# Reordering the first layer: turned output in bank O, memory prepared in steps, branch jobs inside the memory attention, another opening

## The chip, the cores and the metric

The kernel runs on one core of one Trainium2 chip. Its time is the device time of one execution in microseconds (us), and the time before is the median of three runs. Five things of a core matter here: TensorE (PE) multiplies into PSUM banks, VectorE (DVE) and ScalarE (ACT) move and transform data, and the queues of SyncE (SP) and ScalarE issue the DMAs. Each engine takes its instructions strictly in the order in which they were issued to it, and engines wait for each other through semaphores.

## The reference

A transformer block is followed by two layers of another kind, for 512 tokens of width 1024 in float32. The change touches the first block alone:

```python
h = rms_norm(x, norm_mix)
aq, ak, av, bq, bk, bv, cq = split(h @ w_in)            # heads normed, but for the values
out_a = rms_norm(diff_attention(aq, ak, av, slopes_a, lam), a_subln) * (1 - lambda_init)
out_b = softmax-weighted sum of three dilated_window_attention(bq, bk, bv)
m = rms_norm(mem, mem_norm); ck, cv = split(m @ w_mem_kv); ck = rms_norm(ck)
out_c = memory_attention(rms_norm(cq), ck, cv)          # 256 memory tokens
branches = einsum(stack([out_a, out_b, out_c]), w_branch)
gates = sigmoid(h @ w_gate + b_gate)                    # 3 x 1024 columns
x = x + sum(gates * branches) @ w_out
x = x + (silu(h2 @ w_ffn_gate) * (h2 @ w_ffn_up)) @ w_ffn_down
```

## The kernel before

Every large product is made of three matmuls on split operands (high x high, high x low, low x high; `three`, lines 912 to 914). Weights come in units of eight 128x128 tiles (512 KB) through a ring of four buffers. SyncE loads them (L883), ScalarE copies the high part (`whi`, `high`, L1216), VectorE subtracts for the low part (`wlo`, `low`, L1441), and `open_units` puts these two steps into the order two units ahead of their use.

The order of all work is one list, made by hand in `build_schedule` (from L232). Each engine's program walks through that list and issues what the step means to it, so the order of the list is the order of each engine's queue. A step that means nothing to an engine is passed over. A `job` is one column of 128 outputs for all tokens (24 matmuls, 12 for a branch job), in one of three banks, followed by its evacuation `evac` on VectorE. A `group` makes four columns at once for tokens as rows, in four parts (`gpart`, 24 matmuls for x and 12 for the memory), then `gevac`, squares `gsq`, `ginv`, `gnorm`, and the turning `gturn` by PE into bank T0 or O, out of which ScalarE copies. `flush` runs what was deferred after each part or job.

`attend` runs an attention as tiles of 128 queries: `score` (PE, maximum on VectorE, exponential on ScalarE), `probs` (VectorE), `turn` (transposes into T0, copied out by ScalarE) and after four tiles `pv` into bank O. `spread` divides other work, given as pieces, over two slots per tile. The first attention (A) has 16 tiles; its output of each head is normed and turned as a group of its own, `g=("AO", h)`, into `OAH` and `OAL`. Then come the first branch's jobs, the second attention (B), the memory's preparation (`memload`, eight `memfresh`), the second branch (eight jobs with six gate jobs between them), keys and values of the memory (`c_keys`, `c_values`), the memory attention (C) with seven gate jobs as its pieces, the third branch, the reload of x, and `w_out`.

`free[slot]` says for each bank which event a writer has to wait for. For a turned output of attention A it is the end of its low half (L1573), which VectorE writes after ScalarE's high half; for T0 in `turn` it is ScalarE's copy; for O in `pv` it is whatever used O last. The gates' sigmoid (L1340), the exponential (L1355, L1362) and the root (L1305) each load ScalarE's table anew where the function changes.

In the opening, `setup` is the first step: ScalarE issues five constants; PE multiplies a small product of VectorE; then `enter` splits x chunk by chunk (`XH` on ScalarE, `XL` on VectorE, L1489).

## Time and profile before

| | |
|---|---|
| median of 3 runs | 3383.36 us (3381.9 to 3385.7) |
| profiled execution | 3380.15 us |
| its span | 3378.4 us |
| mean granted clock of TensorE | 0.992 |
| busy: PE, VectorE, ScalarE | 3269.1, 1720.1, 1116.2 us |
| HBM read | 309.58 MB, 92 GB/s over the span |

The span runs from the first to the last instruction of the profiled execution. A busy time is the sum over an engine's instructions. In the timeline and the waits, what stands in brackets is how long the engine had been idle before the instruction, and the instruction that released it. The edited places lie in the first 770 us: the opening (0 to 37), the attention A (92 to 262), the second branch (526 to 582), the memory attention (613 to 691), the third branch and `w_out` (691 to 768).

### The profile page before, as it was taken

The numbers are of one execution on the slowest core, as the hardware profiler recorded it, in microseconds if no ns is written. First come the engines' busy times: TensorE is split into PE (matmuls) and PEld (weight loads), VectorE is DVE, ScalarE is ACT, GpSimd is POOL, SyncE is SP. The second block draws the span as 40 slices with busy tenths as digits, with TensorE's granted clock in tenths as the row PEclk, the third lists the DMA queues.
The fourth block names the chain that finished last, engine by engine and source line by source line (L and its number), as shares of the span: only waits on it lengthen the run. The fifth ranks groups of instructions, "written<-read, shape, count | busy, mean of one in ns | idle before, by whom it ended". The sixth has DMA issues, their size and how long they took to land.

```text
span 3378.4 us, 40341 instructions
## 1 busy us (share of the span) xinstructions
PE 3269.1 (97%) x15218; PEld 2683.1 (79%) x15218; DVE 1720.1 (51%) x2485; ACT 1116.2 (33%) x1723; POOL 0.2 (0%) x4
## 2 busy tenths in 40 slices
PE   8899999889999999999999999999999989999998
PEld 7677777678888888888886888888888878688887
DVE  6554445555444445346654545344543666554543
ACT  4554543533222222232333322232223233332221
POOL 0000000000000000000000000000000000000000
PEclk9999999999999999999999999999999999999999
DMA  4223222232222222232221223222223223122222
GB/s 140 94 82 100 92 77 88 87 106 94 96 97 98 96 94 98 96 113 69 88 94 50 99 94 99 94 97 96 97 95 111 80 75 100 63 84 97 97 96 87
DMA packets 88538, 313.43 MB, mean 93 GB/s; under 512 B 9952, under 2 KB 10464, under 8 KB 87904
## 3 DMA queue, kind: packets, MB, share of 16 engines
q1 hardware_dynamic: 82080, 294.69, 26.2%
q10 hardware_dynamic: 6336, 17.03, 1.6%
q8 instruction: 87, 1.43, 0.2%
q14 instruction: 35, 0.29, 0.0%
HBM read 309.58 MB, written 2.10 MB: 92 GB/s over the span
## 4 chain that ended last, share of the span: by engine, by line
PE 90%; DVE 4%; ACT 3%; issue 2%; DMA 1%; DVEq 0%; ACTq 0%; SPq 0%
PE ps L912 28%; PE ps L914 27%; PE ps L913 27%; PE ps L1170 1%; PE ps L1085 1%; ACT stage_sq L1297 1%; PE ps L1063 1%; PE ps L1117 1%; ACT whi L1216 1%; PE ps L1074 1%; PE ps L1100 0%; PE ps L1121 0%; PE ps L1200 0%; PE ps L976 0%; DVE wlo L1441 0%
## 5 line engine op out<-in xcount | busy, mean ns | idle before, releaser
L912 PE MATMUL ps<-x_hi,whi 128*128 128x512 f32 x2400 | 947.5, 395 | 5.0 <-DVE gate_sb L1608 3.5
L914 PE MATMUL ps<-x_hi,wlo 128*128 128x512 f32 x2400 | 937.8, 391 | 0.0
L913 PE MATMUL ps<-x_lo,whi 128*128 128x512 f32 x2400 | 937.8, 391 | 0.0
L1216 ACT ACTIVATE whi<-raw 128x1024 fp32r<-128x1024 f32 x554 | 583.1, 1055 | 969.2 <-DMA raw<-in_weights 966.2
L1441 DVE TENSOR_TENSOR wlo<-raw,whi 128x1024 fp32r<-128x1024 f32 x554 | 676.4, 1223 | 414.8 <-ACT whi L1216 406.5
L912 PEld LDWEIGHTS ps<-x_hi,whi 128*128 128x128 f32 x2400 | 453.3, 189 | 104.0 <-issue 5.2
L914 PEld LDWEIGHTS ps<-x_hi,wlo 128*128 128x128 f32 x2400 | 452.8, 189 | 95.4
L913 PEld LDWEIGHTS ps<-x_lo,whi 128*128 128x128 f32 x2400 | 453.0, 189 | 94.8 <-issue 2.2
L912 PE MATMUL ps<-h_hi,whi 128*128 128x512 f32 x880 | 342.3, 389 | 0.0
L913 PE MATMUL ps<-h_lo,whi 128*128 128x512 f32 x880 | 342.3, 389 | 0.0
L914 PE MATMUL ps<-h_hi,wlo 128*128 128x512 f32 x880 | 342.3, 389 | 0.0
L1725 DVE TENSOR_TENSOR ffn_u<-ps,rstd_x 128x512 f32<-128x512 f32 x110 | 76.0, 691 | 474.7 <-PE ps L914 474.7
L914 PEld LDWEIGHTS ps<-h_hi,wlo 128*128 128x128 f32 x880 | 165.2, 188 | 34.3
L912 PEld LDWEIGHTS ps<-h_hi,whi 128*128 128x128 f32 x880 | 165.2, 188 | 34.3
L913 PEld LDWEIGHTS ps<-h_lo,whi 128*128 128x128 f32 x880 | 165.2, 188 | 34.2
L912 PE MATMUL ps<-whi,x_hi 128*128 128x512 f32 x416 | 168.3, 405 | 3.6 <-DVE wlo L1441 3.2
L1255 ACT ACTIVATE sq<-x_res 128x512 f32<-128x512 f32 x88 | 55.4, 631 | 351.9 <-DVE x_res L1592 301.6
L914 PE MATMUL ps<-whi,x_lo 128*128 128x512 f32 x416 | 163.2, 392 | 0.0
L913 PE MATMUL ps<-wlo,x_hi 128*128 128x512 f32 x416 | 163.0, 392 | 0.0
L1408 ACT ACTIVATE ffn_s<-ffn_g 128x512 f32<-128x512 f32 x110 | 69.6, 632 | 216.2 <-DVE ffn_g L1723 216.2
L1592 DVE SCALAR_TENSOR_TENSOR x_res<-ps,x_res 128x512 f32<-128x512 f32 x72 | 49.8, 691 | 161.1 <-PE ps L914 154.2
L912 PEld LDWEIGHTS ps<-whi,x_hi 128*128 128x128 f32 x416 | 78.9, 190 | 29.2 <-issue 9.3
(274 smaller groups left out, 3415.4 us busy)
## 6 DMA issues: line engine op xcount, KB each, us to landing
raw<-in_weights SPq DMA_DIRECT2D x554, 512.0 KB, 3.3
bias<-in_biasB ACTq DMA_DIRECT2D x16, 384.0 KB, 3.2
bias<-in_biasA ACTq DMA_DIRECT2D x16, 256.0 KB, 3.1
mem_raw<-in_mem ACTq DMA_DIRECT2D x3, 1024.0 KB, 7.5
x_res<-in_x SPq DMA_DIRECT2D x8, 256.0 KB, 6.9
x_res<-in_x ACTq DMA_DIRECT2D x1, 2048.0 KB, 9.5
out_x<-x_res SPq DMA_DIRECT2D x8, 256.0 KB, 2.0
pool_w_sb<-in_pool_w ACTq DMA_DIRECT2D x2, 256.0 KB, 4.9
```

Of the source, the lines that this page charges most:

```text
L912: pe.matmul(out, hi, xhi, start=start, stop=False)
L913: pe.matmul(out, hi, xlo, start=False, stop=False)
L914: return pe.matmul(out, lo, xhi, start=False, stop=stop)
L1063: mm = pe.matmul(sc[:, c * T:(c + 1) * T], AQ[r, h, tt], AK[r, h, :], start=True, stop=True)
L1074: mm = pe.matmul(sc, XQ[:, 2 * h + c, tt], XK[:, 2 * h + c, :], start=(c == 0), stop=(c == 1))
L1085: mm = pe.transpose(out, probs(a)[:, c * P:(c + 1) * P], ident[:, :])
L1216: return act.activation(out, in_, ACT.Copy, scale=scale)
L1255: act.activation(SQ[:, a["sq"], :], X[:, m, :], ACT.Square).then_inc(*sig("sq", (n, m)))
L1408: act.activation(FS[:, :], FG[:, :], ACT.Silu).then_inc(sems["silu"], 1)
L1441: dve.tensor_tensor(wlo[u % RING][:, :], raw[u % RING][:, :], whi[u % RING][:, :].bitcast(F32), ALU.subtract).then_inc(sems["unit_ready"], 1)
L1592: dve.scalar_tensor_tensor(X[:, m, :], out, a["c"], X[:, m, :], ALU.mult, ALU.add)\
L1725: dve.tensor_tensor(FU[:, :], PS[:, 2 * jj + 1, :], RSTD[:, :], ALU.mult).then_inc(sems["fu"], 1)
```

## The change

- The output of attention A is turned in bank O instead of T0.
- Opening: `opening` comes first (ScalarE issues `cols`, VectorE writes zeros, PE makes three matmuls on them), the first unit is loaded and split in halves, and the first part of the first group takes all four token tiles of the first half before those of the second. The constants `ones`, `ident` and `poolrec` are issued at `enter` 3, `halves` is gone, and `setup` stands after the first part.
- The memory's eight `memfresh` steps are put in pairs between the first jobs of the second branch, with gate jobs 2 to 5.
- The second half of the second branch (jobs 4 to 7, gate jobs 6 and 7) becomes four more pieces of the memory attention, before the gate jobs 0 to 6 of the third; gate job 7 follows the attention, and gate job 0 no longer stands before it.
- In the third branch the low half of `y` is its own step `ylo`, one job later.

```diff
 
         def turns():
-            for slot in ("T0", "O"):
+            for slot in ("O", "T0") if isinstance(a["g"], tuple) else ("T0", "O"):
                 if turned:
                     self.step("gturn", c=turned.pop(0), slot=slot, **a)
...
 
-    step("setup")
-    for u, chunks in enumerate(((0,), (1, 2, 3), (4, 5))):
+    step("opening")
+    step("enter", m=0, gain="norm_mix")
+    step("halfunit")
+    step("enter", m=1, gain="norm_mix")
+    s.open_units(0)
+    for u, chunks in ((1, (2, 3)), (2, (4, 5)), (2, (6, 7))):
         for m in chunks:
             step("enter", m=m, gain="norm_mix")
         s.open_units(u)
-    for m in (6, 7):
-        step("enter", m=m, gain="norm_mix")
     a_keys[0]()
     step("consts")
+    step("setup")
     for m in range(4):
         step("refresh", n=0, m=m, gain="norm_mix", entered=True)
...
 
-    def branch(n, o, gate_dst, gates_done):
-        for jj in range(DC // 2):
-            if not gates_done and jj:
-                for m in (2 * jj, 2 * jj + 1):
-                    gate_chunk(n, m, gate_dst(m))
-            t0 = len(s.units) * UT
-            s.unit("w_branch", n, [(k, 2 * jj + mm) for mm in range(2) for k in range(4)])
-            for mm in range(2):
-                m = 2 * jj + mm
-                need = {k: [("olo", ("ABC"[n], k))] for k in range(4)} if m == 0 else {}
-                s.job(t0 + 4 * mm, 4, rhs=o, n=T, evac="branch", b=n, m=m, need=need, gate=gate_dst(m))
+    def branch_pair(n, o, gate_dst, jj):
+        t0 = len(s.units) * UT
+        s.unit("w_branch", n, [(k, 2 * jj + mm) for mm in range(2) for k in range(4)])
+        for mm in range(2):
+            m = 2 * jj + mm
+            need = {k: [("olo", ("ABC"[n], k))] for k in range(4)} if m == 0 else {}
+            s.job(t0 + 4 * mm, 4, rhs=o, n=T, evac="branch", b=n, m=m, need=need, gate=gate_dst(m))
+            if n == 2 and m:
+                step("ylo", m=m - 1)
 
 
     for go in gates_a[5:]:
         go()
     s.drain()
-    branch(0, "OA", lambda m: ("Y", m), True)
+    for jj in range(DC // 2):
+        branch_pair(0, "OA", lambda m: ("Y", m), jj)
     b_work = [b_parts[12:20], b_parts[20:28], b_parts[28:37], b_parts[37:] + [lambda m=m: gate_chunk(1, m, ("GT", m)) for m in range(2)]]
     for h in range(NHEAD):
         attend(b_tiles[h], b_work[h])
...
 
-    for go in memory(0, 0, "mem_norm"):
+    def gate_b(m):
+        gate_chunk(1, m, ("GT", m % 2))
+
+    def pair_b(jj):
+        branch_pair(1, "OB", lambda m: ("GT", m % 2), jj)
+
+    memload, *memparts, memsum = memory(0, 0, "mem_norm")
+    memload()
+    pair_b(0)
+    for k, go in enumerate((lambda: gate_b(2), lambda: gate_b(3), lambda: pair_b(1), lambda: gate_b(4))):
         go()
-    norms, s.norms = s.norms, []
-    branch(1, "OB", lambda m: ("GT", m % 2), False)
-    s.norms = norms
+        memparts[2 * k]()
+        memparts[2 * k + 1]()
+    memsum()
+    gate_b(5)
     gates_c = [lambda m=m: gate_chunk(2, m, ("GC", m)) for m in range(DC)]
-    gates_c[0]()
     attend([dict(kind="C", h=h, t=t, need=[("hq", ("CQ", h)), ("hq", ("CK", h))], need_v=[("gev", (c_group, NM // P - 1))])
-            for h in range(NHEAD) for t in range(NT)], gates_c[1:])
-    branch(2, "OC", lambda m: ("GC", m), True)
+            for h in range(NHEAD) for t in range(NT)],
+           [lambda: pair_b(2), lambda: gate_b(6), lambda: gate_b(7), lambda: pair_b(3)] + gates_c[:7])
+    gates_c[7]()
+    for jj in range(DC // 2):
+        branch_pair(2, "OC", lambda m: ("GC", m), jj)
+    step("ylo", m=DC - 1)
     step("reload")
     norm = 1
...
                 sp.dma_start(X[:, m, :], dram["x"][:, m, :]).then_inc(d_x[m], 16)
-                if m % 2:
+                if m == 0:
+                    sp.dma_start(raw[0][:, 0:4 * P], dram["weights"][0, :, 0:4 * P]).then_inc(sems["d_half"], 16)
+                elif m == 1:
+                    sp.dma_start(raw[0][:, 4 * P:8 * P], dram["weights"][0, :, 4 * P:8 * P]).then_inc(raw_landed[0], 16)
+                elif m % 2:
                     load(0, m // 2)
             with sp.Fori(1, NU // RING) as i:
...
             for kind, a in SCHEDULE.steps:
-                if kind == "setup":
-                    pe.wait_ge(sems["d_cols"], 32)
+                if kind == "opening":
+                    pe.wait_ge(*on("setup", "zeros"))
+                    for _ in range(3):
+                        pe.matmul(O, GSQ[:, 0, 0:P], GSQ[:, 0, :], start=True, stop=True)
+                elif kind == "setup":
...
                     xhi, xlo = parts[a["rhs"]]
-                    pe.wait_ge(sems["unit_ready"], a["unit"] + 1)
-                    for t in range(a["nt"]):
+                    if a["unit"] == 0:
+                        pe.wait_ge(*on("half_ready"))
+                    else:
+                        pe.wait_ge(sems["unit_ready"], a["unit"] + 1)
+
+                    order = [(t, kk) for t in range(a["nt"]) for kk in range(2)]
+                    if a["unit"] == 0:
+                        order.sort(key=lambda at: at[1])
+                    for t, kk in order:
                         b, tt = a["bank"] + t, slice(t * P, (t + 1) * P)
-                        if u == 0:
+                        if u == 0 and kk == 0:
                             if b == 3:
                                 wait_free("T1")
                                 free["T1"] = ("gev", (g, t))
@@ -957,15 +985,16 @@
                             if b in job_in:
                                 pe.wait_ge(*on("evac", job_in.pop(b)))
                             group_in[b] = ("gev", (g, t))
-                        for kk in range(2):
-                            k = 2 * u + kk
-                            if t == 0:
-                                for key in a["need"].get(k, []):
-                                    pe.wait_ge(*on(*key))
-                            w = slice(kk * 4 * P, (kk + 1) * 4 * P)
-                            mm = three(PS[:, b, :], xhi[:, k, tt], xlo[:, k, tt], whi[r][:, w], wlo[r][:, w],
-                                       k == 0, k == DC - 1)
-                        if u == 3 and t < a["nt"] - 1:
+                        k = 2 * u + kk
+                        if t == 0:
+                            for key in a["need"].get(k, []):
+                                pe.wait_ge(*on(*key))
+                            if a["unit"] == 0 and kk == 1:
+                                pe.wait_ge(sems["unit_ready"], 1)
+                        w = slice(kk * 4 * P, (kk + 1) * 4 * P)
+                        mm = three(PS[:, b, :], xhi[:, k, tt], xlo[:, k, tt], whi[r][:, w], wlo[r][:, w],
+                                   k == 0, k == DC - 1)
+                        if u == 3 and kk == 1 and t < a["nt"] - 1:
                             mm.then_inc(*sig("gmm", (g, t)))
                     mm.then_inc(*sig("unit_free", a["unit"]))
...
             for kind, a in SCHEDULE.steps:
-                if kind == "setup":
-                    for t, name, landed in ((cols, "cols", "d_cols"), (ones, "ones", "d_cols"),
-                                            (halves, "halves", "d_consts"), (ident, "ident", "d_consts"),
-                                            (poolrec, "poolrec", "d_consts")):
-                        act.dma_start(t[tuple([slice(None)] * len(t.shape))], dram[name]).then_inc(sems[landed], 16)
+                if kind == "opening":
+                    act.dma_start(cols[:, :], dram["cols"]).then_inc(sems["d_cols"], 16)
+                elif kind == "setup":
                     act.wait_ge(*on("lam_mm"))
                     act.activation(small[:, 2:4], O[:, 0:2], ACT.Exp).then_inc(*sig("lam_exp"))
                     act.wait_ge(*on("setup", "lbd"))
                     act.activation(small[:, 12:20], small[:, 12:20], ACT.Exp).then_inc(*sig("lb_exp"))
+                elif kind == "halfunit":
+                    act.wait_ge(sems["d_half"], 16)
+                    copy(whi[0][:, 0:4 * P], raw[0][:, 0:4 * P]).then_inc(*sig("half_hi"))
+                elif kind == "unit" and a["u"] == 0:
+                    act.wait_ge(raw_landed[0], 16)
+                    copy(whi[0][:, 4 * P:8 * P], raw[0][:, 4 * P:8 * P]).then_inc(sems["unit_hi"], 1)
                 elif kind == "unit":
                     if a["u"] < NU:
                         high(a["u"])
...
                     m = a["m"]
+                    if m == 3:
+                        act.dma_start(ones[:, :], dram["ones"]).then_inc(sems["d_consts"], 16)
+                        act.dma_start(ident[:, :], dram["ident"]).then_inc(sems["d_consts"], 16)
+                        act.dma_start(poolrec[:, :, :], dram["poolrec"]).then_inc(sems["d_consts"], 16)
                     act.wait_ge(d_x[m], 16)
-                    act.wait_ge(sems["d_cols"], 32)
+                    act.wait_ge(sems["d_cols"], 16)
                     copy(XH[:, m, :], X[:, m, :], col(a["gain"], m)).then_inc(*sig("xh", (0, m)))
                 elif kind == "refresh":
...
             for kind, a in SCHEDULE.steps:
-                if kind == "setup":
-                    dve.wait_ge(sems["d_cols"], 32)
+                if kind == "opening":
+                    dve.memset(GSQ[:, 0, :], 0.0).then_inc(*sig("setup", "zeros"))
...
                         .then_inc(*sig("setup", "lam"))
+                elif kind == "halfunit" or kind == "unit" and a["u"] == 0:
+                    half = slice(0, 4 * P) if kind == "halfunit" else slice(4 * P, 8 * P)
+                    dve.wait_ge(*on("half_hi") if kind == "halfunit" else (sems["unit_hi"], 1))
+                    dve.tensor_tensor(wlo[0][:, half], raw[0][:, half], whi[0][:, half].bitcast(F32), ALU.subtract)\
+                        .then_inc(*(sig("half_ready") if kind == "halfunit" else (sems["unit_ready"], 1)))
                 elif kind == "unit":
...
                             dve.tensor_tensor(y, y, g, ALU.add).then_inc(*sig("y", (b, m)))
-                            if b == 2:
-                                dve.wait_ge(*on("yhi", m))
-                                dve.tensor_tensor(YL[:, m, :], y, YH[:, m, :].bitcast(F32), ALU.subtract)\
-                                    .then_inc(*sig("ylo", m))
+                elif kind == "ylo":
+                    m = a["m"]
+                    after_own()
+                    dve.wait_ge(*on("yhi", m))
+                    dve.tensor_tensor(YL[:, m, :], X[:, m, :], YH[:, m, :].bitcast(F32), ALU.subtract)\
+                        .then_inc(*sig("ylo", m))
                 elif kind == "hsum":
                     sum_bank[a["id"]] = a["bank"]
```

## Rows read from the trace of the kernel before

**Rows 1.** The page, part 1: busy us, share of the span and instructions, by engine.

```profile
PE 3269.1 (97%) x15218; PEld 2683.1 (79%) x15218; DVE 1720.1 (51%) x2485; ACT 1116.2 (33%) x1723; POOL 0.2 (0%) x4
```

**Rows 2.** Waits of PE, 0 to 770 us: engine line, waited for, us, times, longest.

```profile
PE ps L1085 <- DVE oa_lo L1573: 12.1, 2, 6.9
```

**Rows 3.** Timeline of PE, opening: start us, us, instruction, count [idle <-releaser].

```profile
10.31 0.79 PE L912 MATMUL ps<-whi,x_hi 128*128 128x512 f32 x1 [3.17 <-DVE wlo L1441]
...
13.94 0.40 PE L912 MATMUL ps<-whi,x_hi 128*128 128x512 f32 x1
...
17.37 0.39 PE L912 MATMUL ps<-whi,x_hi 128*128 128x512 f32 x1
```

**Rows 4.** Timeline, opening, ScalarE (ACT) and VectorE (DVE).

```profile
6.28 0.15 DVE L1453 TENSOR_TENSOR small<-cols 64x2 f32<-64x2 f32 x1 [6.28 <-DMA ones<-in_ones]
...
12.98 1.06 ACT L1216 ACTIVATE whi<-raw 128x1024 fp32r<-128x1024 f32 x1
...
15.00 1.22 DVE L1441 TENSOR_TENSOR wlo<-raw,whi 128x1024 fp32r<-128x1024 f32 x1
...
16.13 1.53 DVE L1489 SCALAR_TENSOR_TENSOR x_lo<-x_res,cols,x_hi 128x512 fp32r<-128x512 f32 x2
```

**Rows 5.** Timeline of PE, 150 to 265 us, at the turned outputs.

```profile
152.77 0.60 PE L976 MATMUL ps<-ident,a_stage 128*128 128x128 f32 x4
160.27 1.09 PE L1085 MATMUL ps<-ident,probs 128*128 128x128 f32 x4 [6.90 <-DVE oa_lo L1573]
...
203.06 1.09 PE L1085 MATMUL ps<-ident,probs 128*128 128x128 f32 x4 [5.22 <-DVE oa_lo L1573]
...
239.79 0.39 PE L1100 MATMUL ps<-a_v,probs_t 128*128 128x128 f32 x2
...
262.09 0.63 PE L976 MATMUL ps<-ident,a_stage 128*128 128x128 f32 x4 [0.87 <-ACT b_q L1216]
```

**Rows 6.** Timeline of ACT and DVE beside them.

```profile
158.67 0.66 ACT L1216 ACTIVATE oa_hi<-ps,cols 128x512 fp32r<-128x512 f32 x1
...
161.39 0.60 ACT L1216 ACTIVATE probs_t<-ps 128x512 f32<-128x512 f32 x1 [0.53 <-PE ps L1085]
...
242.06 0.75 DVE L1573 SCALAR_TENSOR_TENSOR oa_lo<-ps,cols,oa_hi 128x512 fp32r<-128x512 f32 x1 [1.63 <-ACT oa_hi L1216]
```

**Rows 7.** Windows: stretch, us, busy PE, PEld, DVE, ACT, POOL, granted clock, DMA, GB/s.

```profile
200.00:220.00 20.00, 16.94 (x82) 12.63 (x83) 9.51 (x23) 10.07 (x28) 0.00 (x0) 0.83 0.17 52
...
540.00:560.00 20.00, 18.31 (x74) 14.96 (x75) 12.40 (x15) 6.15 (x8) 0.00 (x0) 0.91 0.20 73
```

**Rows 8.** Timeline, first memory preparation, ACT and PE.

```profile
532.58 0.42 ACT L1273 ACTIVATE sq<-mem_raw 128x256 f32<-128x256 f32 x1 [5.57 <-DMA mem_raw<-in_mem]
...
541.69 0.50 PE L912 MATMUL ps<-x_hi,whi 128*128 128x512 f32 x1 [3.53 <-DVE gate_sb L1608]
```

**Rows 9.** Timeline, memory attention, PE and ACT.

```profile
613.64 0.50 PE L912 MATMUL ps<-x_hi,whi 128*128 128x512 f32 x1 [1.49 <-DVE c_v L1542]
...
620.97 1.28 ACT L1362 ACT_TABLE_LOAD   x1
...
622.88 0.70 PE L1071 MATMUL ps<-c_k,c_q 128*128 128x256 f32 x2 [2.62 <-ACT probs L1362]
...
644.15 0.41 PE L1085 MATMUL ps<-ident,probs 128*128 128x128 f32 x2 [1.54 <-ACT probs_t L1216]
...
681.82 0.41 PE L1085 MATMUL ps<-ident,probs 128*128 128x128 f32 x2 [3.20 <-ACT probs_t L1216]
```

**Rows 10.** Timeline of DVE and PE, third branch and w_out; DMA line from the chain.

```profile
699.65 0.69 DVE L1613 TENSOR_TENSOR y_lo<-x_res,y_hi 128x512 fp32r<-128x512 f32 x1 [0.70 <-ACT y_hi L1216]
...
718.70 0.50 PE L912 MATMUL ps<-y_hi,whi 128*128 128x512 f32 x1 [0.98 <-DVE y_lo L1613]
...
721.52 9.49 DMA x_res<-in_x
...
735.46 0.47 PE L912 MATMUL ps<-y_hi,whi 128*128 128x512 f32 x1 [2.07 <-DVE wlo L1441]
```

14 lines of the change are left out of this document (7 added, 7 removed).

## The prediction, made before the change ran

> **What bounds the kernel now.** I read the page first: TensorE (PE) is busy 97% of a span of 3378.4 us [rows 1]. So a change that neither adds nor takes away large matmuls can win only where PE stands idle, 109 us in all, and where its granted clock is at the lower of the two levels. Then I took the PE waits of the first layer, 0 to 770 us: the largest entry is 12.1 us, twice, for one releaser, the low half of a turned output [rows 2]. Then the timeline of each edited place. The clock has a price of its own. In the opening the nine matmuls from 10.31 to 13.94 us are 0.40 us apart, the fifteen from 13.94 to 17.37 are 0.23 apart [rows 3]; the first belong to 1.2 GHz, the second to 2.4. After a long stall the windows show it again: a mean granted clock of 0.91 over 20 us is about 3.5 us at half speed, 1.7 us of lost work; 0.83 is 6.8 us, part of it inside the stall [rows 7]. The stalls of 2.62, 3.20, 3.53, 5.22 and 6.90 us have such a stretch behind them [rows 5, 8, 9], the one of 2.07 us has none [rows 10]. 24 large matmuls, one column job, cost 24 x 0.229 = 5.5 us.
>
> **The turned first output, from bank T0 to bank O.** Before, PE turns head 0's output in T0 at 152.77, and its next instructions, the transposes of a tile's probabilities, need T0 empty. They start at 160.27 after 6.90 us, because the copy out (158.67) stands in ScalarE's queue behind 16 squares [rows 5, 6]. With O they need not wait: they follow at 153.4, the score at 153.9, a weight unit at 155.0 to 160.4. What is late next is the PV of head 1: it needs the copy of the probabilities, which stands behind the same squares, the copy out of O and a square root, and comes at about 161.5 (before 161.39 + 0.60, less the wait for the transposes) [rows 6]. So 1.1 us stay. VectorE then runs 3 us earlier but PE more, so the next turned group finds its copy late by another 1.2 us. Gain: 6.9 + 1.7 (clock) - 1.1 - 1.2 = 6.3 us. Head 1, 203.06: only 8 squares, the copy comes at 204.3 while PE works to 204.9, so 5.22 goes whole, with some 2.5 us of slow work behind it [rows 5, 7]: 7.7 us. Head 2 turns the other way. There the last head's PV follows the turn at once, at 239.79, and PV writes O; its low half is done at 242.06 + 0.75 = 242.81 [rows 5, 6]. Before that cost nothing; now PE waits 3.0 us, plus 0 to 1.7 us of clock (between 2.07, which kept the clock, and 2.62, which lost it, I take 1.1): a loss of 4.1. Head 3: the wait of 0.87 for T0 at 262.09 goes [rows 5]. Sum: 6.3 + 7.7 - 4.1 + 0.9 = **10.8 us gained**, bounds 8 and 13.
>
> **The opening.** Removed from its front: the wait for the second constant, which lands at 6.28 [rows 4], and half of the first unit's conversion (1.06 and 1.22 us for a whole one [rows 4]); I put the first large matmul at 7.3 instead of 10.31 us. Three matmuls on zeros run before it. But "setup" moves behind the first part, and its order counts: VectorE takes it after all eight "enter" steps, PE takes it before the second part and waits there for its first product. The third unit's weights are converted from 12.98, as they land; the bytes ahead of them are nearly the same. On VectorE follow 1.22 us for the low half and 1.53 for the last two x_lo [rows 4]: 12.98 + 1.06 + 1.22 + 1.53 = 16.8, the product at 16.9, PE goes on at 17.2 to 17.4. In the kernel before, the second part starts at 17.37 [rows 3]. PE is done with the first part at 7.3 + 5.5 = 12.8, so the 3 us gained turn into 4.4 us of idle time in front of the second part, and the 3 us at half speed move from the first part, where they would now be covered, to the second: **1.4 us lost**. Bounds: 1.8 lost; 3.0 gained if the product were free (see the rivals). The tables ones, ident and poolrec are issued before the fourth "enter" on ScalarE's queue, 3 issues, covered by the same slack; halves is dropped, never read in the first layer.
> The Trainium skill, Perfetto Trace Analysis, section DMA Optimizations, says that splitting a transfer into smaller ones may let some start sooner and the whole end sooner. By that rule the time would be some 4 us below my sum; by the rows above the start moves and the end of the stage does not.
>
> **Memory in steps.** Before, ScalarE and VectorE stand before the memory (5.57 us on ScalarE), then prepare all eight chunks in a row, and the branch jobs' evacuations wait behind: PE stops 3.53 us at 541.69 [rows 8], clock 0.91 [rows 7]. After, the first chunk comes behind the evacuation of a gate job that PE ends at 538, past the landing at 532.6. Two chunks are some 1.7 us on VectorE between pieces of 5.5 us that need 1.9 (gate) to 4.0 us (two branch jobs) of it, so only the pair of jobs is over by 0.3, and there are banks for two jobs. The last chunk is ready about 3.6 us after the gate job before it, one gate job (5.5) ahead of its first reader. 3.5 + 1.7 = **5.2 us gained**, bounds 3.5 and 5.2.
>
> **Half of the second branch inside the memory attention.** Four pieces of 5.5 us are moved, none added; what counts is the idle time. Before: 1.49, 2.62, 0.84, 1.54, 1.38, 0.40, 0.74, 3.20 and 0.56 us, 12.8 in all (the largest in [rows 9]), and two clock stretches, 3.4 us. After, with 11 pieces over 32 slots instead of 7, I followed the queues: each piece is bounded by what stands in front of the next transposes on ScalarE. At the start no gate and no table load is ahead, but the first maxima wait for two evacuations of c_v: 2.0 us (between 0.9 and the 2.62 of before). After a piece whose sigmoid stands ahead of the copy of the probabilities (gate jobs 7 of the second branch, 0 and 2 of the third) 1.6 us, as the 1.54 at 644.15; once more 0.7 where a PV comes first; 1.3 at the last tile, whose probabilities stand behind an evacuation; 0.3 after the first piece. 2.0 + 3 x 1.6 + 0.7 + 1.3 + 0.3 = 9.1. The 3.20 goes: there a table load and an exponential stood ahead of the copy, and in the new order a tile's copy comes first. Gain 12.8 + 3.4 - 9.1 = 7.1, less 0.6 for a clock stretch that may stay: **6.5 us**, bounds 2 and 10.
> A table load is 1.28 us here [rows 9]. The Trainium skill, ScalarE: Activation LUTs, section What ACT_TABLE_LOAD costs, gives 2.66 us with the drain. With the page's figure the two more gates in the attention would still end inside the next piece, and their sum would be the same to 1 us.
>
> **The third branch and the reload.** Before, each low half y_lo follows its own copy y_hi and VectorE waits 0.70 us for it [rows 10], so a pair of jobs takes VectorE 7.0 us against 5.5 of PE. It falls behind by 4 x 1.5, and PE pays 0.98 us at 718.70 and about 2.1 us three matmuls later; x is reloaded only at 721.52, in 9.49 us, and the fourth column of w_out starts at 735.46 after 2.07 us more [rows 10]. After, y_lo comes one job later: six instructions of 0.72 and one of 1.14 are 5.5 us a pair, PE's own pace. With PE's end of the branch at time 0 (713.3 before) the last y_lo comes at 3.3 instead of 8.2, the reload at 12.8, and the unit that waits behind it 4.3 us later (731.1 to 735.46 before): 17.1 instead of 22.1. **5.0 us gained**, bounds 3 and 5.5.
>
> **Sum.** 10.8 - 1.4 + 5.2 + 6.5 + 5.0 = 26.1 us. The profiled execution took 3380.15 us for a span of 3378.4; its span would be 3352.3, its time 3354. It is 3.2 us below the median of the runs, 3383.36, from which I subtract: **3357.3 us**. The bounds added up give 14.7 to 36.7 us gained, 3346.7 to 3368.7.
>
> **Rivals.**
> *A, the stall only changes its bank.* PV of heads 1 and 2 would wait for O as head 3's does. For it: free["O"] is the low half's end, as T0's was. Against it: PV comes 7 us after the turn there, the low half by 160.2. Price: 3.0 + 1.1 twice, 8 us: 3365.
> *B, the attention stays bound by its own chain.* The copies and exponentials would leave as much idle as before, 12.8 + 3.4. For it: the idle entries there are all released by ScalarE. Against: more matmuls stand between score and transposes. 3357.3 + 6.5 = 3364.
> *C, the opening's gain survives*, if the product is not late. Against: the queue order above. Then 3 us gained instead of 1.4 lost: 3353.
> *D, slower.* In the attention each of the 11 pieces would end as the one at 681.82, 3.20 us and 1.7 of clock [rows 9], 4.9 x 11 = 54 us instead of 9.7: 44 us more, 3402. It decides from a mean of 9.7 / 11 + 26.1 / 11 = 3.3 us per piece. It needs sigmoid, table load and exponential ahead of every copy; only five of the pieces end a gate pair, and the copy is ahead.
>
> **How the numbers follow.** Forecast 62% (3350 to 3363); A 10%; B 12%; C 10%; D 3%; 3% for a loss of all gains by something unseen, near the time before. 0.2%, about what this kernel's measurement can tell, is 6.8 us, so faster means under 3376.6. Forecast, A, B and C are faster: 94%, of which I leave 2 to the other two. The range is 3346 to 3369: the bounds, with A, B and C in it. Faster 0.92, same 0.05, slower 0.03.
>
> **What would show it.** Right: no wait of PE for oa_lo at the probability transposes, one of 3 us at the last head's PV; first large matmul near 7.3 us, then a stall of 4 us ended by the setup product, and the second part at 17.3; no stall between 530 and 560; y_lo without idle time before it, and the reload about 3.3 us behind PE's last branch job. Wrong: a wait on O at heads 1 or 2, idle time over 12 us in the memory attention, or a span less than 15 us shorter.

## The result, and the profile after

The changed kernel takes 3359.91 us (median; 3358.15 to 3361.29) beside 3383.73 us of the kernel before on the same chip, a ratio of 0.9931 with a 95% interval of 0.9915 to 0.9947. The forecast was 3357.3 us, range 3346 to 3369. The profiled execution has a span of 3358.3 us, 20.1 less than before. The page shows a change of idle time, not of work: PE's busy time and its number of instructions are those of [rows 1] to 0.1%. Stretches below are told from one profiled execution of each kernel; after's took 3360.05 us, close to its median.

```profile
span 3358.3 us, 40370 instructions
...
PE 3271.0 (97%) x15224; PEld 2685.5 (80%) x15224; DVE 1720.2 (51%) x2487; ACT 1121.8 (33%) x1729; POOL 0.2 (0%) x4
```

The waits of PE up to 750 us (engine, line, what was waited for, us in total, times, longest): the entry that led before, twice for an oa_lo, 12.1 us in all [rows 2], is gone at the transposes (now L1114). What is left of that releaser stands at the PV product (L1129), once, 3.0 us.

```profile
PE ps L1129 <- DVE oa_lo L1617: 3.0, 1, 3.0
...
PE ps L1005 <- DVE stage L1613: 2.3, 1, 2.3
PE ps L951 <- DVE cols L1496: 2.3, 1, 2.3
PE ps L930 <- DVE wlo L1520: 2.0, 1, 2.0
PE ps L930 <- DVE wlo L1478: 1.9, 1, 1.9
```

To read where the 20.1 us come from I cut PE's timeline of each kernel at the same instructions: the norm sum that ends the opening; the first score of attention A; the first score of attention B (between them lie the turned outputs and the first branch); the first job on OB; the first job on OC (between them the memory preparation and the memory attention); the first and the last matmul on y. Behind the last one all kernels run the same code. All values are us, taken from the timelines.

| kernel | opening, to norm sum | to score A | to score B | to OB | to OC | OC to y | y to last y | unchanged rest |
|---|---|---|---|---|---|---|---|---|
| before | 29.54 | 59.85 | 194.96 | 241.46 | 165.46 | 22.21 | 49.07 | 2615.9 |
| after | 31.84 | 59.88 | 186.61 | 241.44 | 152.07 | 21.76 | 46.88 | 2617.8 |

The terms of the forecast beside these: turned outputs 10.8 forecast, 8.35 measured; opening -1.4 and -2.3; memory in steps with the attention 5.2 + 6.5 = 11.7 and 13.4; third branch with the reload 5.0 and 2.65; unchanged rest 0 and -2.0. Sum 26.1 forecast, 20.1 measured.

**The rest is not constant.** Its code is the same everywhere, yet over the fourteen kernels of this case it took 2612.4 to 2619.3 us. What differs is where stretches at half clock fall. In the timelines the matmuls are then 0.43 us apart instead of 0.23, the two levels of [rows 3]; ahead of its last 10 us the rest of after has five such places, that of before four. So a term under some 3 us can be read only from waits at its own place, and the whole times, whose ratios have an interval of about 5 us to each side, tell only the larger edits apart.

The edited stretches are no more constant than the rest. The kernels of the experiments below have after's code in most of them, and with the same waits of PE (to 0.35 us, but for the opening) they come out at two lengths, as a half-clock stretch or two fall into them or not:

| stretch | before | after | other kernels with after's code in it |
|---|---|---|---|
| opening, to norm sum | 29.54 | 31.84 | 29.44, 30.89, 31.53, 32.24, 32.73, 32.91 |
| score A to score B | 194.96 | 186.61 | 186.15 to 186.69 in six, 184.8 in two |
| OB to OC | 165.46 | 152.07 | 151.9 to 152.1 in six, 155.1 to 155.2 in four |
| y to last y | 49.07 | 46.88 | 46.8 to 47.1 in three, 48.6 to 48.8 in six |

So the measured terms above are those of one profile. With the other lengths the opening's is between -3.4 and +0.1, the turned outputs' 10.1, the memory's and the attention's 10.3, and the third branch's 0.9.

### The profile page after: what moved, and what is told of

Its sections match the earlier page's. It is cut to its first block, busy times and chain, and to the rows that moved or that the text cites. A ratio compares the mean times of both kernels' runs of the same rounds, so it can differ in the third digit from the quotient of the medians.

```text
span 3358.3 us, 40370 instructions
## 1 busy us (share of the span) xinstructions
PE 3271.0 (97%) x15224; PEld 2685.5 (80%) x15224; DVE 1720.2 (51%) x2487; ACT 1121.8 (33%) x1729; POOL 0.2 (0%) x4
## 4 chain that ended last, share of the span: by engine, by line
PE 91%; DVE 4%; ACT 3%; issue 2%; DMA 1%; DVEq 0%; SPq 0%; ACTq 0%
PE ps L930 28%; PE ps L932 27%; PE ps L931 27%; PE ps L1199 1%; PE ps L1114 1%; ACT stage_sq L1334 1%; PE ps L1103 1%; PE ps L1146 1%; ACT whi L1245 0%; DMA x_res<-in_x 0%; PE ps L1229 0%; PE ps L1150 0%; PE ps L1092 0%; PE ps L1005 0%; PE ps L1129 0%
## 5 line engine op out<-in xcount | busy, mean ns | idle before, releaser
L1245 ACT ACTIVATE whi<-raw 128x1024 fp32r<-128x1024 f32 (+1 forms) x555 | 583.3, 1054 | 967.3 <-DMA raw<-in_weights 963.0
```

The source lines that it names most:

```text
L1245: return act.activation(out, in_, ACT.Copy, scale=scale)
```

## The experiments

All kernels are the changed one with the edit shown. First the times, each with the ratio to the kernel before of the same batch (medians of before 3383.7 for after, 3381.9 for the four kernels behind it, 3383.4 for the next four, 3380.6 for the last four).

| kernel | us, median and range | ratio, 95% interval |
|---|---|---|
| after | 3359.9 (3358.2 to 3361.3) | 0.9931, 0.9915 to 0.9947 |
| late_setup | 3358.6 (3353.5 to 3362.9) | 0.9931, 0.9915 to 0.9948 |
| t0_turn | 3369.8 (3367.6 to 3370.2) | 0.9961, 0.9947 to 0.9975 |
| t0_head2 | 3355.0 (3349.1 to 3359.4) | 0.9925, 0.9908 to 0.9942 |
| no_zeros | 3360.5 (3358.4 to 3362.0) | 0.9938, 0.9922 to 0.9955 |
| opening_before | 3356.0 (3354.9 to 3361.7) | 0.9923, 0.9906 to 0.9939 |
| mem_at_once | 3363.6 (3362.1 to 3369.3) | 0.9945, 0.9928 to 0.9961 |
| attn_as_before | 3370.3 (3365.6 to 3374.9) | 0.9956, 0.9939 to 0.9973 |
| ylo_at_once | 3362.1 (3360.2 to 3363.7) | 0.9938, 0.9921 to 0.9954 |
| ylo_pairs | 3358.6 (3354.2 to 3361.0) | 0.9931, 0.9918 to 0.9945 |
| preload | 3358.9 (3356.2 to 3361.0) | 0.9934, 0.9920 to 0.9947 |
| combined | 3351.4 (3348.4 to 3352.2) | 0.9910, 0.9895 to 0.9925 |
| combined_ylo | 3354.2 (3346.9 to 3354.8) | 0.9913, 0.9900 to 0.9927 |

### The turned output: all of it back in T0, and head 2 alone

t0_turn:
```diff
-            for slot in ("O", "T0") if isinstance(a["g"], tuple) else ("T0", "O"):
+            for slot in ("T0", "O"):
```


> The changed kernel with the output of attention A turned in T0 again, all else as changed. Theory: the two waits of 6.9 and 5.2 us at the probability transposes come back with their slow clock, the 3.0 us wait of the last head's PV goes: 8.3 us more than the changed kernel, 3368.2 us. Rival (the stalls there are bound by ScalarE's squares whatever the bank): under 3 us more.

t0_head2:
```diff
-            for slot in ("O", "T0") if isinstance(a["g"], tuple) else ("T0", "O"):
+            for slot in ("O", "T0") if isinstance(a["g"], tuple) and a["g"][1] != 2 else ("T0", "O"):
```


> The changed kernel with head 2 alone turned in T0, the other three in O. Theory: the last head's PV no longer waits 3.00 us for oa_lo and the 3.4 us at half clock behind it go, and T0 has no reader there until 15 us later: 4.7 us less than the changed kernel, 3355.2 us. Rival (something else of that head is as late, such as the copy of the probabilities): a wait of 2 us or more stays and under 1.5 us are gained.

With everything in T0 both stalls come back to the hundredth of [rows 5], and the stretch between the scores is 195.46 us, 8.85 longer than after's 186.61. Timeline of PE, t0_turn (start us, us, instruction, count [idle before <-releaser]):

```profile
163.66 1.09 PE L1114 MATMUL ps<-ident,probs 128*128 128x128 f32 x4 [6.90 <-DVE oa_lo L1617]
...
207.84 1.09 PE L1114 MATMUL ps<-ident,probs 128*128 128x128 f32 x4 [5.22 <-DVE oa_lo L1617]
```

With head 2 alone in T0 the stretch is 180.19 us, 6.4 shorter than after: the 3.00 us wait at the last head's PV goes, and so do the two stretches at half clock that after has between the scores (from 178.7 and from 233.3 us, 3.4 us each). Together that is 3.0 + 2 x 1.7 = 6.4. Only the second of the two stands behind the wait that the edit removes. The first stands behind the 1.87 us at head 1's transposes, which the edit does not touch: t0_head2 still has that wait, at 175.18 us, and keeps its clock behind it, as five kernels do that turn head 2 in O (opening_before, no_zeros, mem_at_once, attn_as_before, ylo_pairs). Windows of t0_head2:

```profile
175.00:185.00 10.00, 9.39 (x48) 6.80 (x48) 6.23 (x14) 8.08 (x14) 0.00 (x0) 1.00 0.31 105
```

So the loss at head 2, shown at its own place, is 3.0 + 1.7 = 4.7 us, and the other 1.7 is not of this edit. The profiled execution of t0_head2, 3349.1 us, is also the fastest of its four. Both median times are near what was expected, 3368.2 and 3355.2, but the interval of t0_head2 lies almost wholly in that of after, and that of t0_turn just touches it.

### The opening: the old one, setup later, no zeros, an early table load

opening_before puts back the whole old front of the schedule and of the engines' "opening" and "enter" steps (no half unit, no zeros, the constants first, "setup" ahead of the x steps), and with it the old order of matmuls in the first part.

> The changed kernel with the opening of the kernel before; turned output, memory, attention and third branch as changed. Theory (the new opening loses, because PE waits for the setup product): the norm's sum comes at 29.5 us as before, 2.3 earlier than in the changed kernel, 3357.6 us. Rival (the new opening gains its 2 to 3 us of earlier start somewhere behind): 3362 us.

late_setup:
```diff
     step("consts")
-    step("setup")
     for m in range(4):
         step("refresh", n=0, m=m, gain="norm_mix", entered=True)
     a_keys[1]()
+    step("setup")
```


> The changed kernel with setup moved one part later: behind the second part of the first group. Theory (queue order): in the changed kernel PE ended the first part near 15.3 us and waited 2.27 us for VectorE's first setup product (17.67), then ran 3.4 us at the lower clock. Without that wait the second part starts at about 15.3, at full clock: 2.7 + 1.7 = 4.4 us less than the changed kernel, about 3355.5 us, and 31.84 (the norm's sum) moves to about 27.5. Rival (the opening is bound by the landing and splitting of x and the units): a wait for unit 1, 2 or x_lo takes its place, and the time stays at 3359.9.

no_zeros:
```diff
-                    for _ in range(3):
-                        pe.matmul(O, GSQ[:, 0, 0:P], GSQ[:, 0, :], start=True, stop=True)
```


> The changed kernel without the three matmuls on zeros in the opening. Theory: they run into the wait for the setup product, which the first part does not set; the first part may run at the lower clock for longer, the wait before the product gets shorter by as much: within 0.7 us of the changed kernel, 3359.9. Rival (they raise the clock for the large matmuls that follow): 1.4 us or more slower, 3361.3.

preload:
```diff
                     act.dma_start(cols[:, :], dram["cols"]).then_inc(sems["d_cols"], 16)
+                    act.wait_ge(*on("setup", "zeros"))
+                    act.activation(small[:, SPARE:SPARE + 1], GSQ[:, 0, 0:1], ACT.Exp).then_inc(*sig("table"))
```


> The changed kernel with one small exponential on zeros at the front of ScalarE's queue, so that the table load no longer waits for x and the table columns (4.51 us) and no longer stands for 1.28 us before the first copy of x. Theory: the first large matmul comes 1 to 1.3 us earlier than 8.04, but the setup product still comes at 17.7, as it hangs on the landing of the third weight unit, so the norm sum stays within 0.7 us of 31.8 except for where a slow stretch of the clock falls, and the time stays at 3360, within 2 us. Rival: the table load is on the path that sets the opening, and the norm sum and the time fall by 1.3 us.

| kernel | first large matmul | second part of the keys | norm sum |
|---|---|---|---|
| before | 10.31 | 17.37 | 29.54 |
| after | 8.04 | 17.95 | 31.84 |
| opening_before | 9.95 | 17.0 | 29.20 |
| late_setup | 8.13 | 15.72 | 28.56 |
| no_zeros | 8.21 | 17.7 | 31.66 |
| preload | 6.43 | 17.8 | 31.79 |

The old opening in the new kernel gives the old norm sum, 29.20, 2.6 us ahead of after's. In the seven kernels with after's opening the norm sum comes at 29.44 to 32.91, with 31.84 in the middle. So the new opening gains nothing, and costs up to 3.4 us beside before's 29.54. In all seven PE's last wait ahead of the second part is for setup's product. The three kernels after, no_zeros and preload start the first part anywhere from 6.43 to 8.21 us and take up the second at 17.7 to 17.95, so the start of the first part does not set it. Timeline of PE, preload; the wait has taken in all that the earlier start gained:

```profile
6.43 0.50 PE L930 MATMUL ps<-whi,x_hi 128*128 128x512 f32 x1 [0.74 <-DVE wlo L1522]
...
17.31 0.56 PE L951 MATMUL ps<-small,ones 64*128 64x2 f32 x2 [5.15 <-DVE cols L1498]
```

late_setup moves that product away and the second part starts 2.2 us earlier; the norm sum comes at 28.56, 3.3 us earlier than after (4.4 were expected) and 0.9 earlier than the earliest kernel with after's opening. There a next wait shows, short in this kernel: the second part waits for all three constant tables, of which poolrec lands last.

```profile
15.72 0.50 PE L930 MATMUL ps<-whi,x_hi 128*128 128x512 f32 x1 [0.49 <-DMA poolrec<-in_poolrec]
```

Its whole time, 3358.6, is not the 3355.5 that was expected, though the interval of 5 us holds both. In its profile the memory stretch is 155.19 us instead of 152.07, with the same waits of PE and two half-clock stretches that after does not have, but preload, ylo_at_once and ylo_pairs do: windows from 565 to 575 and 575 to 585 us, late_setup first, then after (columns as in [rows 7]; the granted clock is the number ahead of the last two):

```profile
565.00:575.00 10.00, 7.75 (x30) 5.74 (x29) 5.50 (x9) 5.88 (x12) 0.00 (x0) 0.83 0.33 105
575.00:585.00 10.00, 8.14 (x31) 6.35 (x30) 6.12 (x14) 5.71 (x11) 0.00 (x0) 0.83 0.30 105
```
```profile
565.00:575.00 10.00, 7.70 (x36) 5.92 (x35) 5.94 (x11) 7.31 (x23) 0.00 (x0) 1.00 0.49 168
575.00:585.00 10.00, 8.13 (x38) 6.47 (x37) 6.99 (x15) 5.53 (x12) 0.00 (x0) 1.00 0.34 107
```

Taking the zeros away changes neither the norm sum nor the time: 31.66 against 31.84, 3360.5 against 3359.9. It may still change the clock of the first part. Of the eleven kernels with the zeros, eight run the whole first part with its matmuls about 0.23 us apart, here mem_at_once, and three, after among them, have six or seven of these steps at 0.43; no_zeros and both kernels with the old opening begin it at 0.43 as well. Windows of mem_at_once:

```profile
8.00:12.00 4.00, 3.96 (x17) 3.30 (x18) 3.27 (x5) 3.10 (x6) 0.00 (x0) 1.00 1.03 401
```

What a faster first part gains goes into the wait for setup's product, 3.38 us there against 2.27 in after. One profile without the zeros in this opening does not show what decides.

### The memory at once, and the attention as before

mem_at_once:
```diff
     memload()
+    for go in memparts:
+        go()
     pair_b(0)
-    for k, go in enumerate((lambda: gate_b(2), lambda: gate_b(3), lambda: pair_b(1), lambda: gate_b(4))):
+    for go in (lambda: gate_b(2), lambda: gate_b(3), lambda: pair_b(1), lambda: gate_b(4)):
         go()
-        memparts[2 * k]()
-        memparts[2 * k + 1]()
```


> The changed kernel with the eight memory steps in a row behind the memory's load, as before. Theory: ScalarE and VectorE stand before the landing again and the branch jobs' evacuations come late: a stall of about 3.5 us with 1.7 of clock, 4 to 5 us more than the changed kernel, 3364.5 us. Rival (the stall came from the queue of gate jobs, not from the memory): within 1 us of 3359.9.

attn_as_before:
```diff
     gate_b(5)
+    for go in (lambda: pair_b(2), lambda: gate_b(6), lambda: gate_b(7), lambda: pair_b(3)):
+        go()
...
     gates_c = [lambda m=m: gate_chunk(2, m, ("GC", m)) for m in range(DC)]
+    gates_c[0]()
...
-           [lambda: pair_b(2), lambda: gate_b(6), lambda: gate_b(7), lambda: pair_b(3)] + gates_c[:7])
-    gates_c[7]()
+           gates_c[1:])
```


> The changed kernel with jobs 4 to 7 of the second branch and its gate jobs 6 and 7 ahead of the keys, and the memory attention with seven pieces as before. Theory: the idle time of the attention is 12 us again instead of 8 and two stretches of low clock come back: 6.5 us more, 3366.4 us. Rival (the waits belong to the tiles' own chain, not to the distance between pieces): under 2 us more.

| kernel | wait for gate_sb | wait for the turned keys | idle in the attention | OB to OC |
|---|---|---|---|---|
| before | 3.53 | 1.36 | 12.8 | 165.46 |
| after | none | 2.28 | 7.35 | 152.07 |
| mem_at_once | 3.38 | 2.19 | 7.33 | 157.35 |
| attn_as_before | none | 3.17 | 12.8 | 165.56 |

mem_at_once costs 5.3 us beside after, the wait of 3.38 and a half-clock stretch behind it, as forecast (5.2). Beside the kernels that take 155.1 us there it would be 2.3, so the 3.38 are what is sure. By the whole times it can't be told from after. Timeline of PE, mem_at_once:

```profile
533.91 0.50 PE L930 MATMUL ps<-x_hi,whi 128*128 128x512 f32 x1 [3.38 <-DVE gate_sb L1652]
```

attn_as_before costs 13.5 us in its profile, twice the 6.5 that were expected. That execution, 3374.9 us, is the slowest of its four; the median, 3370.3, is 10.4 above after's, with intervals that overlap, and leaves room for the 6.5. Its waits are those of before, among them these, which have the lengths of [rows 9]. Timeline of PE, attn_as_before:

```profile
594.76 1.15 PE L1007 MATMUL ps<-ident,stage 128*128 128x128 f32 x4 [3.17 <-DVE stage L1615]
...
605.51 0.50 PE L932 MATMUL ps<-x_hi,whi 128*128 128x512 f32 x1 [1.49 <-DVE c_v L1588]
...
614.75 1.22 PE L1102 MATMUL ps<-c_k,c_q 128*128 128x256 f32 x2 [2.62 <-ACT probs L1401]
...
674.89 0.41 PE L1116 MATMUL ps<-ident,probs 128*128 128x128 f32 x2 [3.20 <-ACT probs_t L1247]
```

Of the 13.5 us, 5.4 are idle time in the attention (12.8 against 7.35) and 0.9 the turned keys. The clock has the rest: windows of attn_as_before from 593 us show 0.83 for 40 us, where after runs at 1.00 in the same attention.

```profile
593.00:613.00 20.00, 15.88 (x60) 12.29 (x60) 10.39 (x15) 7.94 (x12) 0.00 (x0) 0.83 0.23 81
613.00:633.00 20.00, 17.28 (x66) 13.48 (x67) 8.37 (x23) 9.51 (x21) 0.00 (x0) 0.83 0.14 48
```

How far the two edits add is read from the idle time, the sum of the three columns. It is 17.7 us before, 15.9 with the memory in steps alone (attn_as_before), 12.9 with the attention's edit alone (mem_at_once) and 9.6 with both. So the steps take away 1.7 us without the attention's edit and 3.3 with it, as without it 1.8 of the 3.53 come back at the turned keys. The stretches differ by more: by them the steps alone bring nothing (165.56 against 165.46), the attention's edit alone 8.1 us, both 13.4. What lies between is the clock, and with one profile each these runs do not show how much of it belongs to the edits: the same code differs by 3.1 us here.

### The third branch: y_lo at once, y_lo in pairs

ylo_at_once:
```diff
-            if n == 2 and m:
-                step("ylo", m=m - 1)
+            if n == 2:
+                step("ylo", m=m)
...
-    step("ylo", m=DC - 1)
```


> The changed kernel with each y_lo directly behind its y_hi again. Theory: VectorE needs 7.0 us for a pair of branch jobs and falls behind, the reload of x comes about 5 us later: 4.5 us more, 3364.4 us. Rival (the reload's DMA and the unit behind it set the fourth column's start whatever y_lo does): under 1.5 us more.

ylo_pairs:
```diff
-            if n == 2 and m:
-                step("ylo", m=m - 1)
+            if n == 2 and mm:
+                for k in range(max(m - 2, 0), m):
+                    step("ylo", m=k)
```


> Tests why the third branch gave 2.6 us where 5.0 were forecast. In the changed kernel VectorE still needs 6.38 us for a pair of jobs, 0.88 more than PE's 5.5, because the low half of a converted weight unit waits 0.92 us for its high half, which stands on ScalarE behind the copy of y that the second job of the pair lets go. Here the two low halves y_lo of a pair are issued together behind its second job, so that 0.7 us more of VectorE's work stands in that wait. If that wait is the cause, it falls to 0.2 to 0.3 us, a pair takes 5.7 us, the reload is issued about 2.1 us earlier than in the changed kernel relative to PE's last branch job, and the stretch from the first to the last job on y goes from 46.9 to 48.7 us down by 2 us; whole time about 3358 us. Rival: the reload itself or the unit behind it sets the fourth column, and the stretch stays within 0.5 us, the time at 3360.

ylo_at_once brings back idle time of PE for y_lo (1.97 and 1.95 us), issues the reload 9.2 us behind the first job on y instead of 6.0, and has a stretch y to last y of 50.32 us, 3.4 more than after. Of these only 0.9 are idle time; the rest goes with 6.9 us at half clock from 703.2 us on, which after does not have. The whole is 2.2 us above after, less than the 4.5 expected and inside the interval, so it does not decide between the theory and its rival.

The profile of after shows why only 2.65 of 5.0 us came. The copy y_hi is no longer waited for, but a new wait stands in every pair of jobs, at the weight unit. Timeline of VectorE, after, the units of two pairs:

```profile
686.98 1.23 DVE L1478 TENSOR_TENSOR wlo<-raw,whi 128x1024 fp32r<-128x1024 f32 x1 [0.92 <-ACT whi L1245]
...
693.36 1.23 DVE L1478 TENSOR_TENSOR wlo<-raw,whi 128x1024 fp32r<-128x1024 f32 x1 [0.92 <-ACT whi L1245]
```

They are 6.38 us apart where PE needs 5.5. The high half whi stands on ScalarE behind the pair's second y_hi, which VectorE itself lets go only with x_res. In ylo_pairs one y_lo more lies over that wait, and units are 5.66 us apart:

```profile
687.27 1.22 DVE L1479 TENSOR_TENSOR wlo<-raw,whi 128x1024 fp32r<-128x1024 f32 x1 [0.20 <-ACT whi L1246]
...
692.93 1.23 DVE L1479 TENSOR_TENSOR wlo<-raw,whi 128x1024 fp32r<-128x1024 f32 x1 [0.19 <-ACT whi L1246]
```

PE's wait for y_lo of 1.03 us is gone, the reload is issued 4.5 us behind the first job on y instead of 6.0, and the stretch y to last y is 45.76 instead of 46.88. The cause is shown; the size is 1.1 us, not 2, since the reload now waits for three y_lo in a row. The whole time (3358.6) does not tell it from after.

### The edits together

combined is late_setup, t0_head2 and preload in one kernel; combined_ylo adds ylo_pairs.

> Three edits of the changed kernel together: setup's product behind the second part of the keys, head 2's turned output alone back in T0, and the early table load. Each removes a stall of its own place: if they add, the norm sum comes at 27.3 us instead of 31.8 (4.5 us, of which the table load is 1.2), the turned outputs' stretch is 180.2 instead of 186.6 us (6.4 us), and the time is 3359.9 - 10.9 = 3349. Rival: the first of them is undone by where the clock's slow stretches fall later, as when it was made alone (3358.6 instead of 3355.5), and the time is 3353 to 3355, no less than with head 2 alone.

> The three edits and the two low halves of y together behind each pair of the third branch. If all places are independent, 2 us less than the three together, about 3347 us. Rival: nothing is left at the reload, and it is within 0.7 us of the three together.

| kernel | opening | to score A | to score B | to OB | to OC | OC to y | y to last y | rest |
|---|---|---|---|---|---|---|---|---|
| t0_head2 | 29.44 | 59.79 | 180.19 | 241.44 | 152.01 | 21.76 | 48.61 | 2614.1 |
| combined | 30.92 | 59.73 | 181.66 | 241.57 | 152.02 | 21.76 | 47.13 | 2615.5 |
| combined_ylo | 30.46 | 59.75 | 181.74 | 242.68 | 151.91 | 21.76 | 45.36 | 2619.3 |

combined is the fastest median: 3351.4, 0.9910 of before, and 0.0021 below after's ratio, which is 7 us where 10.9 were expected; the two intervals still overlap. The turned outputs keep their gain, 4.95 us beside after. The opening does not: its norm sum was expected at 27.3 and comes at 30.92. Timeline, combined: the issue of poolrec on ScalarE's queue, and PE.

```profile
9.94 0.45 ACTq L1284 DMA_DIRECT2D poolrec<-in_poolrec  x1
...
16.55 0.79 PE L930 MATMUL ps<-whi,x_hi 128*128 128x512 f32 x1 [3.94 <-DMA poolrec<-in_poolrec]
```

The first part starts at 6.87 and is done at 12.6. Then "consts", in which PE waits for all three tables, holds the second part until poolrec lands, 6.6 us behind its issue, though the keys read none of it; and PE comes out of that wait at half clock (1.5 us lost). The 0.49 us in late_setup was the same wait, nearly covered. So neither theory of the opening was complete: once setup is away, a table's landing is late next, and the earlier start of preload goes into that wait. An edit that lets PE wait for that table at its first reader was not tried.

combined_ylo shortens y to last y by 1.8 us more, and its rest is 3.8 us longer; its time can't be told from combined's.

## Why the prediction was right, point by point

**The bound** held: work stayed the same to 0.1%, and the whole gain is idle time and clock in the first layer.

**The turned output** (10.8 forecast, 8.35 measured). The long waits moved where the prediction said: PV of head 1 waits 0.90 us (1.1 forecast), the last head's PV 3.00 (3.0), and the 5.22 at 203 us went whole. Timeline of PE, after:

```profile
163.74 3.84 PE L1129 MATMUL ps<-a_v,probs_t 128*128 128x128 f32 x32 [0.90 <-ACT probs_t L1245]
...
177.66 0.63 PE L1114 MATMUL ps<-ident,probs 128*128 128x128 f32 x4 [1.87 <-DVE probs L1718]
...
233.11 3.15 PE L1129 MATMUL ps<-a_v,probs_t 128*128 128x128 f32 x16 [3.00 <-DVE oa_lo L1617]
```

The term mis-sized is what follows: at 177.66 I took 1.2 us and it is 1.87, with half-clock matmuls behind it that the sum did not have (1.7); the stretch behind the 3.00 costs 1.7, not 1.1. That is 0.7 + 1.7 + 0.6 = 3.0, a little more than the miss of 2.45. In attn_as_before and ylo_pairs, with the same waits, the 1.7 behind the 1.87 is not lost, and the stretch is 184.8: a gain of 10.1. My bound that a stall of 2.07 us leaves the clock alone was no rule: 1.87 did not here.

**The opening** (1.4 lost forecast with bounds of 1.8 lost and 3.0 gained, 2.3 lost measured; the old one in its place shows 2.6). The order of queues was read rightly: the product is the late one, the second part forecast at 17.2 to 17.4 and measured at 17.95, behind the product's matmul at 17.67. Rival C, that the gain survives, is refuted: no kernel with this opening has its norm sum more than 0.1 us ahead of before's, and in preload the wait takes in the whole of a still earlier start. Two sizes were off. The first large matmul comes at 8.04, not 7.3, as the table load has moved ahead of the first copy of x. ScalarE, after:

```profile
4.51 1.28 ACT L1245 ACT_TABLE_LOAD   x1 [4.51 <-DMA cols<-in_cols]
5.80 0.72 ACT L1245 ACTIVATE x_hi<-x_res,cols 128x512 fp32r<-128x512 f32 x1
```

Before, it ran from 3.13 us, under the landing of the constants. Here it costs nothing, as preload shows, since the product comes later still. And PE runs slow twice, with a stall of 2.27 us between instead of the 4.4 forecast: windows of after, granted clock 0.57, 1.00 and 0.59. The prediction had the slow stretch move from the first part to the second. That is what five of the other six kernels with this opening do, and the sixth, t0_head2, is slow in the first part alone, waits 0.79 us and has its norm sum at 29.44.

```profile
8.00:12.00 4.00, 3.96 (x10) 3.13 (x11) 2.78 (x4) 2.39 (x4) 0.00 (x0) 0.57 1.01 395
12.00:16.00 4.00, 3.40 (x15) 2.44 (x13) 3.84 (x6) 3.77 (x6) 0.00 (x0) 1.00 0.76 284
18.00:22.00 4.00, 4.00 (x12) 3.18 (x12) 3.31 (x14) 3.62 (x8) 0.00 (x0) 0.59 0.29 120
```

The split of the first unit gave what the rows of before let one expect: PE starts 2.3 us earlier, and the stage ends no earlier. The Trainium skill, Perfetto Trace Analysis, section DMA Optimizations, says that where the DMA engines are generally idle, smaller transfers may let the whole task end sooner. Here they are not idle, with a DMA share of 1.01 from 8 to 12 us above, and no run here shows an earlier end from the split. Of the table load the Trainium skill, ScalarE: Activation LUTs, section What ACT_TABLE_LOAD costs, says 1.28 us and 1.38 more for a drain; the rows above show the 1.28, and the next instruction 0.01 us behind its end.

**Memory in steps and the attention** (11.7 forecast, 13.4 measured, 10.3 in the four kernels that take 155.1 us). The stall of 3.53 is gone; between 540 and 560 us PE is busy all 20.00 us at clock 1.00, against 18.31 at 0.91 [rows 7]:

```profile
540.00:560.00 20.00, 20.00 (x92) 16.59 (x91) 14.55 (x25) 12.39 (x20) 0.00 (x0) 1.00 0.34 114
```

Idle time in the attention was forecast at 9.1 and is 7.35 in six waits, of which these are the first, which is the longest, and one of the two of 1.32:

```profile
582.63 0.70 PE L1100 MATMUL ps<-c_k,c_q 128*128 128x256 f32 x2 [1.87 <-ACT probs L1399]
...
620.20 0.41 PE L1114 MATMUL ps<-ident,probs 128*128 128x128 f32 x2 [1.32 <-ACT probs_t L1245]
```

So 2.0 for the start was right (1.87), and what I put at 1.6 behind a sigmoid is 1.32 or less. The wait at the turned keys, 1.36 before and 2.28 now, was not in the sum. It balances: idle 3.53 + 1.36 + 12.8 = 17.7 before, 2.28 + 7.35 = 9.6 after, so 8.1; three half-clock stretches fewer, 5.1; together 13.2 of the 13.4. What failed is that I priced the two edits as independent: in idle time the steps are worth 1.7 us alone and 3.3 beside the other edit, the attention's edit 4.8 and 6.3. By the lengths of the stretches it would be 0.1 and 5.3, 8.1 and 13.5, with the clock's own changes in them. That the sum of the two terms came close is in part luck, since the same code also took 3.1 us more. Rival B would have left 12.8 us idle and D 3.2 behind every piece; with 7.35 in all, both are refuted.

**The third branch and the reload** (5.0 forecast with bounds of 3 and 5.5, 2.65 measured). The wrong step is the pace of a pair: "six instructions of 0.72 and one of 1.14 are 5.5 us". I counted VectorE's work and no wait; the 0.92 at the weight unit makes it 6.38. Three pairs later that is 3 x 0.88 = 2.6 us, and the last y_lo ends 5.95 us behind PE's end of the branch (693.60) instead of 3.3. The rest of that chain stands: reload 9.4 us, the column 4.3 us behind VectorE's first instruction on the landed x (713.41 - 709.09). With 5.95 in its place it gives 19.8, as measured, and before 22.0. Six other kernels with the same code there run 3.4 us at half clock behind the wait at the fourth column; they take 48.6 to 48.8 us from y to last y, and of the term 0.9 us is left.

```profile
699.58 9.38 DMA x_res<-in_x
...
713.41 0.47 PE L930 MATMUL ps<-y_hi,whi 128*128 128x512 f32 x1 [1.95 <-DVE wlo L1478]
```

**The sum** came 6 us too high by the spans (26.1 against 20.1), 2.3 us by the medians (26.1 against 23.8). A third of the miss by the spans, 2.0 us, is in code that the change does not touch, where half-clock stretches fell otherwise. The opening and the third branch lie outside their own bounds, and the memory's and the attention's term came out above its forecast, so the whole is closer than its parts. The miss of 2.6 us on the time is also less than the 6.9 us by which the unchanged rest alone differs among the profiles, so that it is so small is in part luck. Two numbers of the prediction were misread or misadded, without weight in its sum: before, the second wait for y_lo is 1.87 us, not about 2.1, and rival D adds up to 3401.5, not 3402. **Rival A** is refuted: no wait on O at heads 1 or 2.

## What to carry to other kernels

When a wait is removed, follow each queue for the wait that is late next, in the pace of a loop as much as at a stall: here a semaphore for constants that nobody nearby reads and a copy queued behind another took back up to 3.9 and 2.6 us. Turning every output into the other bank was right for the heads whose transposes follow at once and wrong for the one whose PV follows at once; decide the bank by the next reader in each place. Where a kernel's clock moves between its levels, judge an edit of a few microseconds by the waits at its own place, not by the whole time, and not by the length of a stretch in one profile either: look first how far that length differs among kernels with the same code in it.

## What the runs showed of the hardware that was not expected

The same instructions with the same waits did not always run at the same clock. The wait of 1.87 us for the probabilities in attention A has half-clock matmuls behind it in after (window 175 to 185 us: 0.83), and the same wait of 1.86 us in ylo_pairs has none (160 to 180 us: 1.00; no slow matmul up to 230). In the memory attention after keeps 1.00 behind waits of 2.28 and 1.87 us where late_setup and three other kernels lose 3.1 us behind the same ones. What decides between them was not found; no run here isolates it.

```profile
175.00:185.00 10.00, 8.13 (x34) 5.84 (x33) 6.23 (x15) 8.82 (x16) 0.00 (x0) 0.83 0.29 105
```
```profile
160.00:180.00 20.00, 17.24 (x97) 12.96 (x96) 13.76 (x31) 14.53 (x36) 0.00 (x0) 1.00 0.23 79
```

Three matmuls on zeros ahead of the first real ones did not always keep the clock: in after, late_setup and t0_head2 six or seven steps of the first part are 0.43 us, in the eight others with the zeros none is. And a small table was slow to land while much else was in flight: poolrec, 32 KB, lands 6.6 us behind its issue in combined, beside transfers of 287 to 434 GB/s in the half-microsecond slices of that stretch, where the masks, 448 KB, issued at 15.25 us near that stream's end, land in 3.6. That the stream is the cause is argued from this, not tested.
